# Layer 0's imaginary drive table turned by VectorE in feed-forward chunks, with GpSimd's tables in another order

## The reference

```python
h = h + 0.5 * swiglu(rmsnorm(h), w_gate, w_up, w_down)       # D_FF = 2816
z = rmsnorm(h) @ w_in
y_a = z_b * (causal_conv3(z_c * z_v) + conv_b)
y_s = s5_group(z_s, ...)
h = h + concat(rmsnorm(y_a), rmsnorm(y_s)) @ w_out
h = h + 0.5 * swiglu(rmsnorm(h), ...)
h = h + (p[i] @ w_ple) * sigmoid(rmsnorm(h) @ w_gate)
```

```python
lb = exp(A * dt)                         # complex, from A_re, A_im, log_dt
bb = (lb - 1) / A * B                    # complex: bb_re, bb_im
state[t] = lb * state[t-1] + bb @ u[t]   # an associative scan
y = Re(C @ state) + D * u
```

## Time and profile before

| | us |
|---|---|
| median of three timed runs (995.86 to 996.42) | 996.39 |
| the profiled execution | 995.49 |
| its span | 993.7 |
| TensorE busy | 981.0 |
| VectorE busy | 862.5 |
| ScalarE busy | 515.4 |
| GpSimd busy | 365.7 |

### The profile page before, as it was taken

How to read it: one execution, slowest core, us unless ns; L and a number is a source line. 1 busy time by engine, 2 the same in 40 slices (tenths; PEclk the granted TensorE clock), 3 DMA queues, 4 the chain that set the end, 5 groups by cost and what they waited for, 6 DMA issues and landing times.

```text
span 993.7 us, 16217 instructions
## 1 busy us (share of the span) xinstructions
PE 981.0 (99%) x5549; PEld 832.4 (84%) x5549; DVE 862.5 (87%) x1482; ACT 515.4 (52%) x760; POOL 365.7 (37%) x554
## 2 busy tenths in 40 slices
PE   8999999999999999999999999999999999999996
PEld 7888888899988888888878888889998888888885
DVE  7898999899889888996789978997998898787874
ACT  6544444584854443445564444445856454444463
POOL 6888999710137889970009500002002100000000
PEclk9999999999999999999999999999999999999998
DMA  9766564533647855554636555554444565655541
GB/s 283 229 211 211 169 211 169 171 128 129 209 133 225 239 181 200 169 211 170 212 128 212 182 198 171 209 177 134 158 170 148 191 212 174 206 185 195 204 157 43
DMA packets 143745, 181.64 MB, mean 183 GB/s; under 512 B 18448, under 2 KB 125648, under 8 KB 143696
## 3 DMA queue, kind: packets, MB, share of 16 engines
q1 hardware_dynamic: 142512, 179.42, 54.5%
q10 hardware_dynamic: 1184, 1.59, 0.5%
HBM read 179.93 MB, written 1.05 MB: 182 GB/s over the span
## 4 chain that ended last, share of the span: by engine, by line
PE 96%; DVE 2%; DMA 1%; issue 1%; ACT 1%; SPq 0%; POOL 0%; POOLq 0%; DVEq 0%
PE ps L1602 30%; PE ps L1603 30%; PE ps L1604 30%; PE ps L1617 1%; DVE wL L872 1%; DMA raw<-in_ffn_w_up_dram 1%; PE ps L1905 1%; PE ps L1871 0%; PE ps L1935 0%; PE ps L1929 0%; DVE uL L902 0%; PE ps L1915 0%; PE ps L1766 0%; ACT bufB L665 0%; PE ps L1943 0%
## 5 line engine op out<-in xcount | busy, mean ns | idle before, releaser
L872 DVE TENSOR_TENSOR wL<-raw,wH 128x1024 fp32r<-128x1024 f32 x334 | 426.5, 1323 | 21.4 <-ACT wH L471 20.2
L471 ACT ACTIVATE wH<-raw 128x1024 fp32r<-128x1024 f32 x334 | 335.3, 1052 | 101.6 <-PE ps L1604 90.8
L1602 PE MATMUL ps<-wH,uH 128*128 128x512 f32 x832 | 326.2, 392 | 3.1 <-DVE wL L872 1.6
L1604 PE MATMUL ps<-wH,uL 128*128 128x512 f32 x832 | 324.0, 389 | 0.0
L1603 PE MATMUL ps<-wL,uH 128*128 128x512 f32 x832 | 323.8, 389 | 0.0
L971 DVE STREAM_TRANSPOSE hTf<-bufB 32x128 f32<-32x128 f32 x640 | 193.7, 303 | 9.5
L1602 PEld LDWEIGHTS ps<-wH,uH 128*128 128x128 f32 x832 | 156.2, 188 | 37.2 <-DVE wL L872 2.4
L1604 PEld LDWEIGHTS ps<-wH,uL 128*128 128x128 f32 x832 | 156.2, 188 | 32.8
L1603 PEld LDWEIGHTS ps<-wL,uH 128*128 128x128 f32 x832 | 156.3, 188 | 31.4
L1602 PE MATMUL ps<-wH,hTH 128*128 128x512 f32 x352 | 137.9, 392 | 0.0
L1604 PE MATMUL ps<-wH,hTL 128*128 128x512 f32 x352 | 137.1, 389 | 0.0
(11 more groups left out here) (204 smaller groups left out, 1061.2 us busy)
## 6 DMA issues: line engine op xcount, KB each, us to landing
raw<-in_ffn_w_down_dram SPq DMA_DIRECT2D x88, 512.0 KB, 4.0
raw<-in_ffn_w_gate_dram SPq DMA_DIRECT2D x86, 512.0 KB, 4.0
raw<-in_ffn_w_up_dram SPq DMA_DIRECT2D x86, 512.0 KB, 5.0
raw<-in_w_in_dram SPq DMA_DIRECT2D x32, 512.0 KB, 4.4
raw<-in_w_out_dram SPq DMA_DIRECT2D x16, 512.0 KB, 4.2
raw<-in_ple_w_gate_dram SPq DMA_DIRECT2D x16, 512.0 KB, 4.2
raw<-in_glu_w_dram SPq DMA_DIRECT2D x4, 512.0 KB, 3.7
raw<-in_ple_w_proj_dram SPq DMA_DIRECT2D x4, 512.0 KB, 3.8
```

The lines of the kernel that those rows point to most:

```text
L471: nc.scalar.activation(wH[:, slot, w], raw[:, slot, w], ACT.Copy).then_inc(wh_done, 1)
L872: nc.vector.tensor_tensor(wL[:, slot, w], raw[:, slot, w], wH[:, slot, w].bitcast(F32), ALU.subtract).then_inc((wl_half, wl_done)[a], 1)
L1602: mul(o, sH, vH, start=start, stop=False)
L1604: return mul(o, sL, vH, start=False, stop=stop)
```

## The change

- `EI_EARLY` goes; both layers take layer 1's way. VectorE turns layer 0's Ei after chunks 6 to 9 of its first feed-forward; TensorE's second set of `turn_E` and its four evacuations go.
- `setup_E` computes bb and E right after the powers, ahead of the rotation tables, in both layers. It raises `ei_ready` once for each finished time step, the last one (s = 3) first, and `drive_tables` at its end.
- `turn_Ei` takes s = 3, 2, 1, 0 and waits for `ei_ready` in place of `ssm_ready`.
- pa, pb, bbr and bbi move from regT to bufA, columns 0 to 1535. Since bufA then holds scratch, ScalarE waits in `embedding` of layer 0 for `drive_tables` of layer 1 before it writes pp.
- `drive(0)` stands ahead of k step 4 of the second half of unit 1, in both layers.

```diff
-E_BANKS = ((6, 7, 2, 3), (6, 7, 3, 5))
+E_BANKS = (6, 7, 2, 3)
-EI_EARLY = (1,)
...
-        bbr = regT[:, 2048:2304].rearrange("p (b h) -> p b h", b=NB)
-        bbi = regT[:, 2304:2560].rearrange("p (b h) -> p b h", b=NB)
-        pa = regT[:, 2560:3072].rearrange("p (b h) -> p b h", b=NB)
-        pb = regT[:, 3072:3584].rearrange("p (b h) -> p b h", b=NB)
+        bbr = bufA[:, 0:256].rearrange("p (b h) -> p b h", b=NB)
+        bbi = bufA[:, 256:512].rearrange("p (b h) -> p b h", b=NB)
+        pa = bufA[:, 512:1024].rearrange("p (b h) -> p b h", b=NB)
+        pb = bufA[:, 1024:1536].rearrange("p (b h) -> p b h", b=NB)
...
             def embedding(l):
+                if l + 1 < DEPTH:
+                    act.wait_ge(drive_tables, l + 2)
                 for q in range(4):
...
             def turn_Ei(l, s):
-                if s == 0:
-                    dve.wait_ge(ssm_ready, l * 2 + 2)
+                dve.wait_ge(ei_ready, l * T + (T - s))
...
-                early = f == 0 and l in EI_EARLY
-                with dve.Fori(2, EI_CHUNKS[0] if early else NFC - 1) as i:
+                with dve.Fori(2, EI_CHUNKS[0] if f == 0 else NFC - 1) as i:
                     step(i)
-                if early:
-                    for s, i in enumerate(EI_CHUNKS):
+                if f == 0:
+                    for n, i in enumerate(EI_CHUNKS):
                         step(i)
-                        turn_Ei(l, s)
+                        turn_Ei(l, T - 1 - n)
...
                 scaled_u(l, 0)
-                if l not in EI_EARLY:
-                    E_turned(l, 1, 1)
                 drive_in(l, 0)
-                if l not in EI_EARLY:
-                    E_turned(l, 1, 3)
...
                 csquare(v(A4R), v(A4I), v(A2R), v(A2I), v(TMP), v(W))
+                pool.wait_ge(b_ld, (l + 1) * (16 * NB_B))
+                cmul([(bbr, whole)], [(bbi, whole)], over_h(FR), over_h(FI), br, bi, pah, pbh)
+                for o, src in ((Er, bbr), (Ei, bbi)):
+                    for part, sl in halves(o, T - 1):
+                        link(g.tensor_copy(part, src[sl]))
+                pool.sem_inc(ei_ready, 1)
+                for k in range(1, T):
+                    n_r, n_i = powers[k]
+                    cmul(halves(Er, T - 1 - k), halves(Ei, T - 1 - k), over_h(n_r), over_h(n_i), bbr, bbi, pah, pbh)
+                    pool.sem_inc(ei_ready, 1)
...
-                pool.wait_ge(b_ld, (l + 1) * (16 * NB_B))
-                cmul([(bbr, whole)], [(bbi, whole)], over_h(FR), over_h(FI), br, bi, pah, pbh)
...
+                pool.sem_inc(drive_tables, 1)
...
                 w_in_unit(l, 0, {(1, 3): lambda: spread_scale(l)})
-                if l not in EI_EARLY:
-                    for b in range(4):
-                        turn_E(l, 1, b)
-                w_in_unit(l, 1, {(1, 2 if l in EI_EARLY else 0): lambda: drive(0)})
+                w_in_unit(l, 1, {(1, 4): lambda: drive(0)})
```

More of the change, by code:

```diff
@@ L229, in trunk @@
         etd_done, eti_done = sem("etd_done"), sem("eti_done")
+        ei_ready, drive_tables = sem("ei_ready"), sem("drive_tables")
         kt_ps, kt_done = sem("kt_ps"), sem("kt_done")
@@ L526, in mixer_norm @@
                 squares(l, 1, 1)
-                E_turned(l, 0, 0)
+                E_turned(l, 0)
                 act.wait_ge(kc_ps, l + 1)
                 nc.scalar.activation(kcf, ps[:, 0, :], ACT.Copy).then_inc(kc_done, 1)
-                E_turned(l, 0, 2)
+                E_turned(l, 2)
                 def diagonals():
@@ L538, in mixer_norm, with E_turned @@
                 nc.scalar.activation(rsb[:], ps[:, 4, 0:SEQ], ACT.Copy).then_inc(rsb_done, 1)
-                if l not in EI_EARLY:
-                    E_turned(l, 1, 0)
-            def E_turned(l, r, b):
-                if r == 0 and b == 0:
+            def E_turned(l, b):
+                if b == 0:
                     act.wait_ge(ssm_ready, l * 2 + 2)
-                act.wait_ge(et_ps, l * 8 + (4 * r + b + 1))
-                nc.scalar.activation((ETr, ETi)[r][:, 4 * b:4 * b + 4, :],
-                                     ps[:, E_BANKS[r][b], :].rearrange("p (b c) -> p b c", b=4),
+                act.wait_ge(et_ps, l * 4 + (b + 1))
+                nc.scalar.activation(ETr[:, 4 * b:4 * b + 4, :], ps[:, E_BANKS[b], :].rearrange("p (b c) -> p b c", b=4),
                                      ACT.Copy).then_inc(et_done, 1)
@@ L710, in mixer @@
                 drive_in(0)
-                if l not in EI_EARLY:
-                    E_turned(l, 1, 2)
                 act.wait_ge(rsb_done, l * 2 + 1)
@@ L931, in into_mixer, with E_turned @@
                 parts(l, 1, 3)
-                E_turned(l, 0, 1)
-                E_turned(l, 0, 3)
+                E_turned(l, 1)
+                E_turned(l, 3)
                 split_at(l, U_IN + 1)
                 half_split(l, U_IN + 2, (U_IN + 2) % SLOTS, 0)
-            def E_turned(l, r, b):
-                if r == 0 and b == 1:
+            def E_turned(l, b):
+                if b == 1:
                     dve.wait_ge(ssm_ready, l * 2 + 2)
-                dve.wait_ge(et_ps, l * 8 + (4 * r + b + 1))
-                nc.vector.tensor_copy((ETr, ETi)[r][:, 4 * b:4 * b + 4, :],
-                                      ps[:, E_BANKS[r][b], :].rearrange("p (b c) -> p b c", b=4)).then_inc(etd_done, 1)
+                dve.wait_ge(et_ps, l * 4 + (b + 1))
+                nc.vector.tensor_copy(ETr[:, 4 * b:4 * b + 4, :],
+                                      ps[:, E_BANKS[b], :].rearrange("p (b c) -> p b c", b=4)).then_inc(etd_done, 1)
             def hidden(l, f, i, between=None):
@@ L1548, in mixer @@
                 pool.wait_ge(kc_full, l + 1)
-                pool.wait_ge(et_ps, l * 8 + (4 if l in EI_EARLY else 8))
+                pool.wait_ge(et_ps, l * 4 + 4)
                 for state in (Sr, Si):
@@ L1858, in w_in_unit, with turn_E @@
                 last.then_inc(wt_used, 1)
[L1860 to L1868, removed]
+            def turn_E(l, b):
+                if b >= 2:
                     pe.wait_ge(ul_done, low_at(l, 1, b - 2, 3))
                 for j in range(4):
-                    last = nc.tensor.transpose(ps[:, E_BANKS[r][b], j * P:(j + 1) * P],
-                                               (Er, Ei)[r][:, 4 * b + j, :, :].rearrange("p s c -> p (s c)"), ident[:])
+                    last = nc.tensor.transpose(ps[:, E_BANKS[b], j * P:(j + 1) * P],
+                                               Er[:, 4 * b + j, :, :].rearrange("p s c -> p (s c)"), ident[:])
                 last.then_inc(et_ps, 1)
@@ L1896, in drive @@
                     pe.wait_ge(rsb_done, l * 2 + 1)
[L1897 to L1900, removed]
+                    pe.wait_ge(et_done, l * 2 + 2)
+                    pe.wait_ge(etd_done, l * 2 + 2)
+                    pe.wait_ge(eti_done, (l + 1) * T)
                     for p in range(4):
@@ L1952, in mixer @@
                 for b in range(4):
-                    turn_E(l, 0, b)
+                    turn_E(l, b)
                 turn_taps(l)
                 w_in_unit(l, 0, {(1, 3): lambda: spread_scale(l)})
-                if l not in EI_EARLY:
-                    for b in range(4):
-                        turn_E(l, 1, b)
-                w_in_unit(l, 1, {(1, 2 if l in EI_EARLY else 0): lambda: drive(0)})
+                w_in_unit(l, 1, {(1, 4): lambda: drive(0)})
                 turn_drive(0)
```

## The result

The changed kernel takes 1001.81 us (median of five runs, 1001.3 to 1004.64); the kernel before takes 996.39 (five runs, 995.37 to 996.61). The ratio is 1.0061, with a 95% interval of 1.005 to 1.0072. The change makes the kernel slower by 5.4 us. The kernel before was run again for the experiments and then took 995.8 us (median of 26) and 995.74 (of 16); against these the changed kernel, which was not run again, is 6.0 us slower. The profiled execution after took 1001.81 us with a span of 1000.0, so the two profiled spans differ by 6.3 us.

A forecast was written before the change was run, and what follows sets the result against it. TensorE, busy for 99% of the span, was taken to bound the kernel. Lag +8.2, transposes -1.75 and layer 1's drive -0.45 gave +6.0 on the median 996.39, 1002.4, stated as 1002.2 us, range 998.9 to 1004.6.

The forecast's parts named there:

- the lag: TensorE's delay through layer 0's first feed-forward from four added VectorE turns: 8.2 us, bounds 6 to 9.5.
- VectorE is at its limit in layer 0 because GpSimd slows its subtractions: Layer 0's feed-forward: a weight unit's subtraction costs 3.28 us beside GpSimd, 2.36 in layer 1; transposes show no loss.
- The lead is 2.2 us, used up by one turn: Layer 0: weights of gate_up(7, 1) ready 2.2 us early; after one turn gate_up(8, 1) has lag 0.
- the 0.4 us for narrow GpSimd operations in chunk 6: Layer 0, chunk 6: E moved earlier leaves GpSimd at narrow operations near 121 us, saving VectorE about 0.4 us.
- The lags at the down units: Layer 0: TensorE late by 1.8 us at down(7), 4.9 at down(8), 7.8 at down(9), 8.3 at the last hidden turn.
- 1.75 us for the transposes: Layer 0's mixer: sixteen Ei transposes leave TensorE's chain, gaining 1.75 us, bounds 1.3 to 1.9.
- late next is drive(0): Layer 0's mixer, transposes gone: drive(0) is the next late piece, waiting at most 0.2 us for VectorE's placement of u.
- 0.45 us for layer 1's drive: Layer 1's mixer: two more k steps ahead of drive(0) fill TensorE's idle time, gaining 0.45 us, bounds 0 to 0.6.
- Nothing from the reorder, the scratch and drive_tables: GpSimd's new order, scratch in bufA and the new waits cost 0; ScalarE's pp wait has 34 us of cover.
- Covered, as in layer 1: Rival: layer 0's turns cost TensorE nothing, as in layer 1's 16.40 us chunks; -2.2 us, 994.2; chance 0.08.
- Half covered: Rival: GpSimd ends near 170 us, not 187, so the lag is 3 us less: 999.4; chance 0.12.
- More lag: Rival: stalls make something else late or TensorE's clock falls, price 3 us: 1005.4; chance 0.06.

The follow-up runs named there:

- the third experiment: The changed kernel without GpSimd's products of G in layer 0, so GpSimd is idle from about 154 us, all turns kept: 997.26 us, ratio 1.0014.
- The second experiment on the drive: The kernel before with drive(0) ahead of k step 4 of unit 1's second half in both layers, nothing else: 995.76 us, ratio 1.0001.
- the first experiment: The kernel before with only GpSimd's E ahead of the rotation tables, scratch in bufA and ScalarE's wait for drive_tables: 995.65 us, ratio 0.9999.

## Why the prediction was right

The total came out as forecast, 1001.81 against 1002.2, inside the range, and the mechanism is the one named. That it came so close is in part luck: the lag was put 0.4 us too high (8.2, measured 7.79) and the gains 0.46 too high (2.2, measured 1.74), so the sum, +6.0, met the 6.05 of the profiles with two errors in it; and the two medians differ by 5.4, the two profiled spans by 6.3. By its steps:

- *VectorE is at its limit in layer 0 because GpSimd slows its subtractions.* Right: 3.28 us a unit beside GpSimd, 2.31 to 2.36 in the same chunk of the same layer when GpSimd is stopped (the third experiment). The transposes keep their 0.703 us.
- *The lead is 2.2 us, used up by one turn.* Right, and the lead was a little less than that: the silu of chunk 7 comes on time at 131.61, that of chunk 8 is already 1.1 us late, where I had 0 for gate_up(8, 1). Its wL ended at 140.43 + 2.78 = 143.2, less 0.28 for the start 142.9; I had 142.2. Another 0.2 is that TensorE had begun this gate_up at 142.01 before, not at 142.2. The term that was mis-sized is the 0.4 us for narrow GpSimd operations in chunk 6: wL 2.64, hTL 1.15 and 6.49 us after, against 2.56, 0.88 and 6.57 before, so nothing was saved there.
- *The lags at the down units.* wL down(7) ended at 146.74 + half of 5.69, 149.6, less 0.28: lag 1.7 (forecast 1.8). wL down(8): 165.64 + 3.3 = 168.9, less 0.28: 4.7 (4.9). wL down(9): 187.73, less 0.28: 7.2 (7.8). The last hidden turn: 190.84 - 182.98 - 0.28 = 7.6 (8.3). The first agrees since two errors cancel: chunk 6 saved nothing, but in chunk 7 hTL took 0.69 and two units 5.69 us, against 1.23 and the 6.57 that I had carried over. GpSimd's timeline at that time:

```profile
146.15 1.89 POOL L1345 TENSOR_TENSOR prm<-prm 128x16 f32<-128x16 f32 x2
148.11 1.90 POOL L1503 COPY decay<-prm 128x1008 f32<-128x1008 f32 x1
```

It was at narrow operations and at a copy, where before it had been at E's wide products. The reorder had changed VectorE's neighbour, and a duration carried over from the same place before was not that of the same company. At the end hTL took 0.69 us at 183.67 and two units 5.71 at 184.28, where I had carried over 1.10 and 6.59; GpSimd stops at 186.6. That is most of why the lag ends at 7.6 and not 8.3.
- *GpSimd ends near 187.* Its last row starts at 183.78 and takes 2.85 us: 186.6. *Ei ready near 113*: 109.1.
- *The silus.* I had said 18 to 19 us apart for chunks 7 to 10. They are 17.42, 18.48 and 19.20 us: the mean fits, but they grow from chunk to chunk.
- *1.75 us for the transposes.* The step that failed is "late next is drive(0)". drive(0) had its data in time in both layers, as forecast. But ScalarE's chain behind it was late next: evacuation, taps and second placement, with 1.1 us spare before. TensorE's work ahead of drive(1) shrank by 1.75 us, ScalarE's evacuation moved up by only 0.4 us, since drive(0) itself now stands four k steps later. 1.1 - 1.35 leaves 0.25 us of wait. 1.52 was inside its bounds, 1.3 to 1.9.
- *0.45 us for layer 1's drive.* The wait ahead of drive(0) goes, as forecast; the same new wait takes half of it. Measured 0.22; bounds 0 to 0.6. The second experiment on the drive shows that place alone does this.
- *Nothing from the reorder, the scratch and drive_tables.* Right, by the first experiment. ScalarE's pp evacuation after shows no wait for GpSimd: it starts at 481.89, 6.5 us later than before like everything around it.
- *The rivals.* "Covered, as in layer 1" is what the third experiment makes true from 154 us on, and there a chunk costs 16.41 us. "Half covered" had GpSimd end near 170; it ended at 186.6. "More lag" by a falling clock didn't come: 1.00 in all three windows.

The Trainium skill's rule on the lock ("SBUF — State Buffer", Who interferes with whom), by which a VectorE instruction with two SBUF inputs contends with GpSimd's reads and one with a single SBUF input doesn't, is borne out by the third experiment too. When GpSimd had stopped, two wL units took 4.62 us instead of 6.55; the hidden transposes took 5.05 us and the four of a turn 2.85 as before.

The version that this points to is the kernel before with layer 1's drive at k step 3; the timed runs can't tell it from the kernel before. Layer 0's Ei is better left with TensorE: 1.5 us there against a lag of 4.7 in the cheapest place that was tried for VectorE.

## What to carry to other kernels

An in-order engine that is busy for 95% of each round has little more than its lead to give: write down, for each piece that the bounding engine needs, when it is ready and when it is needed, and add the new work ahead of it; here that gave the lag of 7.8 us to within 0.5. The same work can cost TensorE next to nothing in one layer (16.40 us a chunk) and 7.8 us in another, where a third engine slows the one that takes it. When TensorE's work ahead of a wait shrinks, ask for the whole queue of each engine up to the next thing that TensorE needs, not only for the first.

## What the runs showed of the hardware

That VectorE's transposes are not slowed by GpSimd (0.703 us each, beside it and without it) while its subtractions are, by 39% (3.28 against 2.36 us a unit), was in the trace of before; that the subtractions are back at 2.36 us in the very chunk in which GpSimd stops was new. Stalls of TensorE that add up to 0.9 and 2.9 us in chunks of 18 to 20 us, none longer than 1.54 us, left the granted clock at 1.00. In the profile of the kernel without layer 0's turns the granted clock was 0.50 (1.2 GHz) from 9 to 12 us, and TensorE had been idle for 1.80 us up to 7.81; in the kernel before and in the third experiment it had been idle for 1.43 and 1.55 us at the same place, and the clock stayed at 1.00. Those three profiles alone don't show what made it fall.
